# Four pairs of norm rows: 128-partition loads against one row, a product with ones and a ScalarE copy

## The chip, the cores and the metric

The kernel runs on one core of a Trainium2 chip, in float32 throughout. The metric is the device time of one execution in microseconds. Where several executions were timed, their median is given.

## The reference, cut to what matters

The model is a stack of two blocks on 256 tokens of width 1024. The first block (two hybrid layers) comes before the part in question. The second block has two layers, each an attention mixer and a mixture of 32 experts, of which every token takes two:

```python
for i in range(DEPTH):                       # DEPTH = 2
    mod = c_act @ ada_w[i] + ada_b[i]
    sh1, sc1, g1, sh2, sc2, g2 = jnp.split(mod[:, None, :], 6, axis=-1)
    h = x * (1 + sc1) + sh1
    y = mixer(h)                             # neighbourhood (i=0) or grouped-query (i=1)
    x = layer_norm(DEEPNORM_ALPHA * x + (1 + g1) * y, ln_g[i, 0], ln_b[i, 0])
    h = x * (1 + sc2) + sh2
    y = hierarchical_moe(h, ...)             # 32 experts, 1024 -> 512 -> 1024, gated by SiLU
    x = layer_norm(DEEPNORM_ALPHA * x + (1 + g2) * y, ln_g[i, 1], ln_b[i, 1])
```

`ln_g` and `ln_b` are rows of 1024 numbers, 4 KB each. A norm multiplies every token by the same row, and tokens lie on partitions, so the row is needed on all 128 partitions. There are four norms in the second block, so eight rows. Each expert has 6 MB of weights, 192 MB a layer, and all experts' weights are read.

## The kernel before, in words

One program is written out for each engine (TensorE, VectorE, ScalarE, GpSimd, SyncE); counting semaphores join them. Each engine works its own list strictly in order, so a wait holds up all that is behind it on that engine.

A layer of experts has this order. The mixer's output (`output(i)`) turns the tokens, computes the logits and normalizes. The `router(i)` picks the experts: on TensorE it makes the second gates (`second_gates`, a product of one row with ones, two halves in layer 0 and one in layer 1), then `busy`, a number of warming products whose results nobody reads (`busy(2 + i, 4)`; the profile shows two and three, as `busy` is called with i = 0 and 1), then, once VectorE has the choice (semaphore `asg`), the products that give each token its rank in an expert (`pos`) and the counts (`ct`). VectorE turns the ranks into a selection.

Then `experts(i)` goes over 8 quads of four experts (`q` from 0 to 7). A quad has a gather (tokens to expert slots, PSUM banks 0 and 1, taken out half by ScalarE and half by VectorE), the gate and up products (L910) of the four experts, turns of the hidden values (`hidden`), the gather of the next quad, two halves of down products (`down(0)`, `down(1)`, L946) and two of combining products (`combine`, L956). In the last quad the order is `down(0)`, `combine(0)`, `down(1)`, `combine(1)`.

The weights pass through nine slots of 2 MB: five of the tile `ring` and four in the arena `AR`. SyncE issues the loads in a fixed order and, for each, waits until the slot's former piece has been used. The plan `PARTS` lets the first three pieces of a layer free their slots in parts. The last quad's down weights are in pieces of 1 MB, by half.

The norm rows are loaded by GpSimd, whose queue has the function `small` for it (L2214). `norm_before(i)` loads the pair of the norm ahead of the experts (`LN_IN`: bias first, then scale), when the mixer's tokens are ready; `finish(i)` on GpSimd multiplies and adds them while the experts run, and signals `fin`. `norm_after(i)` loads the pair of the norm behind the experts (`LN_OUT`), scale when TensorE has filled the last gate products of quad 6, bias after those of quad 7; `last_norm(i)` on VectorE uses them. `LN_IN[1]`, `LN_OUT[0]` and `LN_OUT[1]` lie where gathered tokens lie at other times, `LN_IN[0]` where the scaled outputs lie. `begin` and `end` on TensorE reserve a PSUM bank and signal that it is filled; `free` signals that it is drained.

Of the kernel before, what the change touches and what calls it, by code (L numbers as in the profile page):

```python
# [10 lines left out]
ACT = mybir.ActivationFunctionType  # L11
AX = mybir.AxisListType.X

P = 128
NT = 2
D = 1024
# [114 lines left out]
def program(nc, A, out):  # L131
    with ExitStack() as ctx:
# [5 lines left out]
        def sem(name):  # L138
            if name not in sems:
                sems[name] = ctx.enter_context(nc.semaphore("s_" + name))  # L140
            return sems[name]
# [277 lines left out]
        def _(eng):  # L419
# [444 lines left out]
            def second_gates(i, j):  # L864
                pe.wait_ge(*drained("adaT", 12 * i + 10 + j))
                gate_rows("g2", i, 1, j, 1 if j and not i else 7)

            def router(i):
                for j in range(2 - i):
                    second_gates(i, j)  # L870
                busy(2 + i, 4)
                up = cst[:, K_UP:K_UP + 128]
                o = begin(4, "pos", i)
                pe.wait_ge(sem("asg"), i + 1)
                eng.matmul(o[:, 0:32], up, R_ASG[:, 0, :], start=True, stop=True)
                end(product(o[:, 32:64], [(up, R_ASG[:, 1, :]), (ones[:, :], R_ASG[:, 0, :])]), "pos", i)
                o = begin(7, "ct", i)
                end(product(o[:, 0:32], [(ones[:, :], R_ASG[:, 0, :]), (ones[:, :], R_ASG[:, 1, :])]), "ct", i)

            def experts(i):  # L880
# [9 lines left out]
                        end(ins, "xg", i, q, b)  # L890

                gather(0)
                for q in range(NQ):
                    u = q % 2

# [33 lines left out]
                    hidden(3)  # L929
                    if q + 1 < NQ:  # L930
                        gather(q + 1)

                    def down(n):
                        o = begin(5 + n, "dn", i, q, n)
# [24 lines left out]
                    down(0)  # L959
                    if q == NQ - 1:  # L960
                        combine(0)
                        down(1)
                    else:
                        down(1)
                        combine(0)
# [61 lines left out]
        def _(eng):  # L1027
# [794 lines left out]
            def last_norm(i):  # L1822
                for t in range(NT):
                    deviation(t)
                v.wait_ge(sem(f"row{2 * i + 1}"), 32)
                for t in range(NT):
                    v.step(stt(X[:, t, :], X[:, t, :], bn_a[:, t, 0:1], LN_OUT[0], ALU.subtract, ALU.mult))
                v.chain()
                for t in range(NT):
                    v.wait_ge(sem("lrs"), n_dev[0] - 1 + t)  # L1830
                    ins = stt(X[:, t, :], X[:, t, :], st2[:, t:t + 1], LN_OUT[1], ALU.mult, ALU.add)
                    if i + 1 < DEPTH:
                        v.tell(ins, sem("xn"), 3 + t)
                    else:
                        v.tell(ins, sem("xl"), t + 1)
# [12 lines left out]
        def _(eng):  # L1848
# [192 lines left out]
            def output(i):  # L2041
# [2 lines left out]
                raw_cols(i, 1)  # L2044
                normed(i, 1)

            def second_gates(i, j):
                s.wait_ge(*filled("g2", i, j))
                free(act(G2[j], bank("g2", i, j)[:, :], ACT.Copy), "g2", i, j)
# [82 lines left out]
            def router(i):  # L2132
                for j in range(2 - i):
                    second_gates(i, j)
                s.chain()
                eg, e2 = rt(104, NT, 4), rt(90, NT)
                s.wait_ge(sem("eg"), i + 1)
# [4 lines left out]
            def experts(i):  # L2142
# [12 lines left out]
                            s.step(ins)  # L2155

                gather(0)
                for q in range(NQ):
                    for j in range(4):
                        n = 32 * i + 4 * q + j  # L2160
# [7 lines left out]
                        second_gates(i, 1)  # L2168
                    if q + 1 < NQ:
                        gather(q + 1)  # L2170

            def overflow(i):
                o_pe, o_v, o_s = sem(f"o_pe{i}"), sem(f"o_v{i}"), sem(f"o_s{i}")
# [29 lines left out]
        def _(eng):  # L2203
# [20 lines left out]


            def norm_row(k, n, dst):
                small(dst, A[("ln_g", "ln_b")[n]][k // 2, k % 2:k % 2 + 1, :].to_broadcast([P, D]), f"row{k}")

            def norm_before(i):
                g.wait_ge(*drained("o", TAG[i], 7))  # L2230
# [16 lines left out]


            def finish(i):
                g.wait_ge(sem(f"row{2 * i}"), 32)  # L2250
                g.wait_ge(sem("sel"), 8 * i + 1)
                x = [X[:, t, :].rearrange("p (k c) -> p k c", c=NC) for t in range(NT)]
                for t in range(NT):
# [294 lines left out]
```

## Time and the profile before

| what | value |
|---|---|
| runs: median (lowest to highest of 3) | 1555.37 us (1554.26 to 1557.9) |
| profiled execution: span from first to last instruction | 1548.5 us |
| profiled execution: its own time | not listed in the views, which give its span alone |
| TensorE matmul, busy | 1384.9 us, 89% |
| VectorE busy | 563.6 us, 36% |
| ScalarE busy | 214.9 us, 14% |
| GpSimd busy | 88.4 us, 6% |
| DMA, hardware queue of SyncE | 519.40 MB, 83.2% of 16 engines |
| DMA, software queue of GpSimd | 11.95 MB, 2.2% of 16 engines |
| mean granted TensorE clock | 0.957 |

A product of float32 shows as two or more matmul instructions, and matmuls are pipelined, so TensorE's busy share says little by itself. A DMA share of one means that all 16 engines are working. PE is TensorE, PEld its weight loads, DVE VectorE, ACT ScalarE, POOL GpSimd, SPq SyncE's queue of instructions. A bracket after a row tells how long the engine idled before it and who ended that.

### The profile page before, as it was taken

Reading aid. Unit: us, or ns where it says so; the run is one execution under the profiler, and the core shown is the slowest. Engines: PE = TensorE matmul, PEld = TensorE weight load, DVE = VectorE, ACT = ScalarE, POOL = GpSimd, SP = SyncE. Lnnn points to the kernel's source line nnn. Section 1 sums busy time; section 2 is a strip of 40 time slices with the busy share of each in tenths; the row PEclk is TensorE's granted clock in tenths of the full one; section 3 lists DMA queues with packets and bytes.
Section 4 is the critical chain, followed back from the end, with each engine's and each line's share of the span. In section 5 each row is a group of like instructions: output and inputs, shape, how many; then the busy total and the mean of one; then the engine's idle time right before and its main releaser. Section 6 shows DMA issues by size and latency. Waiting matters only on the chain.

```text
span 1548.5 us, 28441 instructions
## 1 busy us (share of the span) xinstructions
PE 1384.9 (89%) x12810; PEld 880.9 (57%) x12810; DVE 563.6 (36%) x1254; ACT 214.9 (14%) x574; POOL 88.4 (6%) x95
## 2 busy tenths in 40 slices
PE   7999999999999999879879787879999798798795
PEld 4886478678886556435445343457765363454451
DVE  3696459656753321111111115794111111111113
ACT  2230123012332000000000002442100000000000
POOL 3100111000003000000000001100200000000000
PEclk9999999999999999989989899989999898899898
DMA  9656845767769999999999999357999999999995
GB/s 346 219 192 231 307 163 179 273 241 268 272 274 389 415 426 426 427 427 426 428 425 427 426 379 337 110 202 279 423 409 426 427 427 427 427 426 426 425 418 200
DMA packets 98296, 533.33 MB, mean 344 GB/s; under 512 B 5344, under 2 KB 7584, under 8 KB 74352
## 3 DMA queue, kind: packets, MB, share of 16 engines
q1 hardware_dynamic: 94432, 519.40, 83.2%
q0 software_dynamic: 3728, 11.95, 2.2%
q8 instruction: 105, 1.72, 0.4%
q14 instruction: 31, 0.25, 0.1%
HBM read 530.28 MB, written 1.05 MB: 343 GB/s over the span
## 4 chain that ended last, share of the span: by engine, by line
PE 66%; DMA 26%; DVE 4%; SPq 2%; issue 1%; ACT 1%; DVEq 0%; ACTq 0%
PE bk L438 28%; PE bk L910 17%; DMA ring<-in_moe_w_down 16%; DMA AR<-in_moe_w_down 9%; PE bk L946 8%; PE bk L619 4%; PE bk L956 4%; PE bk L434 2%; SPq L2356 2%; PE bk L648 1%; PE bk L663 1%; DVE AR L1031 1%; ACT AR L1852 1%; DMA ring<-in_w_in 1%; DVE AR L1039 1%
## 5 line engine op out<-in xcount | busy, mean ns | idle before, releaser
L910 PE MATMUL bk<-ring,AR 128*32 128x128 f32 x4480 | 267.7, 409 | 4.4 <-DMA ring<-in_moe_w_up 4.4
L1031 DVE TENSOR_TENSOR AR<-bk,AR 128x128 f32<-128x128 f32 (+2 forms) x106 | 41.3, 390 | 517.4 <-ACT AR L1852 451.5
L910 PEld LDWEIGHTS bk<-ring,AR 128*32 128x32 f32 x4480 | 178.8, 127 | 83.8 <-DMA ring<-in_moe_w_up 6.9
L910 PE MATMUL bk<-AR 128*32 128x128 f32 x3712 | 223.4, 409 | 3.5 <-DMA AR<-in_moe_w_up 2.8
L438 PE MATMUL bk<-ring,AR 128*128 128x256 f32 (+2 forms) x736 | 210.6, 444 | 6.5 <-ACT AR L1852 2.9
L946 PE MATMUL bk<-ring,AR 128*32 128x512 f32 x608 | 158.9, 696 | 51.4 <-DMA ring<-in_moe_w_down 50.6
L1852 ACT ACTIVATE AR<-bk 128x512 f32<-128x512 f32 (+4 forms) x178 | 72.0, 422 | 928.6 <-PE bk L910 757.5
L910 PEld LDWEIGHTS bk<-AR 128*32 128x32 f32 x3712 | 145.0, 127 | 74.1 <-DMA AR<-in_moe_w_up 5.9
L438 PEld LDWEIGHTS bk<-ring,AR 128*128 128x128 f32 x736 | 139.6, 192 | 71.4 <-issue 54.4
L946 PE MATMUL bk<-AR 128*32 128x512 f32 x416 | 149.6, 693 | 29.5 <-DMA AR<-in_moe_w_down 29.5
L438 PE MATMUL bk<-AR,ring 128*128 128x256 f32 (+1 forms) x832 | 170.5, 364 | 1.7 <-DVE AR L1036 1.4
L438 PEld LDWEIGHTS bk<-AR,ring 128*128 128x128 f32 x832 | 147.5, 190 | 21.6 <-issue 3.4
L946 PEld LDWEIGHTS bk<-ring,AR 128*32 128x32 f32 x608 | 35.0, 125 | 129.0 <-DMA ring<-in_moe_w_down 73.3
L1031 DVE TENSOR_TENSOR AR<-bk,mpart 128x512 f32<-128x512 f32 x32 | 22.1, 692 | 222.6 <-PE bk L946 222.6
L1039 DVE SCALAR_TENSOR_TENSOR mpart<-ring,ccol,mpart 128x512 f32<-128x512 f32 x126 | 98.7, 784 | 4.5
L434 PE MATMUL bk<-cst,AR 128*128 128x128 f32 (+1 forms) x356 | 63.9, 292 | 27.0 <-DVE AR L1699 11.8
L434 PEld LDWEIGHTS bk<-cst,AR 128*128 128x128 f32 (+1 forms) x356 | 41.3, 142 | 62.2 <-issue 26.2
L946 PEld LDWEIGHTS bk<-AR 128*32 128x32 f32 x416 | 31.8, 124 | 75.8 <-DMA AR<-in_moe_w_down 43.1
L438 PE MATMUL bk<-AR 128*128 128x128 f32 (+1 forms) x536 | 68.9, 286 | 1.0 <-DVE AR L1031 1.0
L438 PEld LDWEIGHTS bk<-AR 128*128 128x128 f32 x536 | 63.8, 193 | 5.2 <-issue 3.1
L956 PE MATMUL bk<-AR 128*128 128x512 f32 x128 | 59.7, 606 | 3.3 <-DVE AR L1031 3.3
L1031 DVE TENSOR_TENSOR X<-X,bk 128x512 f32<-128x512 f32 x64 | 44.0, 688 | 40.1 <-PE bk L619 23.9
(154 smaller groups left out, 947.9 us busy)
## 6 DMA issues: line engine op xcount, KB each, us to landing
ring<-in_moe_w_gate SPq DMA_DIRECT2D x36, 2048.0 KB, 28.8
ring<-in_moe_w_up SPq DMA_DIRECT2D x34, 2048.0 KB, 26.4
AR<-in_moe_w_up SPq DMA_DIRECT2D x30, 2048.0 KB, 29.7
AR<-in_moe_w_gate SPq DMA_DIRECT2D x28, 2048.0 KB, 26.8
ring<-in_moe_w_down SPq DMA_DIRECT2D x28, 2048.0 KB, 34.4
ring<-in_ada_w SPq DMA_DIRECT2D x24, 2048.0 KB, 10.8
AR<-in_moe_w_down SPq DMA_DIRECT2D x22, 2048.0 KB, 34.2
ring<-in_w_in SPq DMA_DIRECT2D x12, 2048.0 KB, 12.8
```

The costliest lines, as they stand in the source:

```text
L434: return eng.transpose(o, a, ident[0:k, 0:k])
L438: ins = eng.matmul(o, l, r, start=i == 0, stop=i == len(pairs) - 1)
L619: ins = eng.matmul(o[:, :], BIG[:, x, OUTS[m] + 128 * t:OUTS[m] + 128 * t + 128], w[:, 2 * m + x, :], start=k + x == 0, stop=k + x == 4)
L648: ins = eng.matmul(o[b][:, a * nk:(a + 1) * nk], g["q"][h][:, t * 128:(t + 1) * 128], g["k"][h][:, 0:nk], start=True, stop=True)
L663: ins = eng.matmul(o[64 * b:64 * b + 64, 128 * x:128 * x + 128], g["v"][2 * x + b][kt], ET[j % 2][:, (2 * b + x) * nkt + kt, :], start=kt ...
L910: ins = eng.matmul(o[32 * f:32 * f + 32, 128 * m:128 * m + 128], XG[u][:, c, 32 * j:32 * j + 32], w[:, c, f::4], start=c == 0, stop=c == N ...
L946: ins = eng.matmul(o[32 * j:32 * j + 32, :], AT[u][:, j, 32 * f:32 * f + 32], w, start=f == 0, stop=f == 3)
L956: end(eng.matmul(o[:, :], GST[u][:, 128 * t:128 * t + 128], YS[:, 512 * n:512 * n + 512], start=True, stop=True), "cb", i, q, n, t)
L1031: return eng.tensor_tensor(o, a, b, op)
L1039: return eng.scalar_tensor_tensor(out=o, in0=a, scalar=s, in1=b, op0=op0, op1=op1)
L1852: return eng.activation(o, a, f, **kw)
L2356: eng.dma_start(dst, src).then_inc(sem(f"slot{s}"), 16)
```

## The change

The eight rows are no longer loaded to 128 partitions, 512 KB each. GpSimd loads each to partition 0 alone, 4 KB, at the same places of its list. TensorE multiplies a column of ones with the row, in two halves of 512 columns, which puts the row on all partitions of a PSUM bank, and ScalarE copies each half to the place where the 512 KB load put it. The users (`finish`, `last_norm`) wait for these copies. On TensorE the pairs of products stand: LN_IN[1] in the router behind the second gates, with one warming product fewer; LN_IN[0] behind the first gather; LN_OUT[0] behind the last quad's hidden values, ahead of `down(0)`; LN_OUT[1] between `combine(0)` and `down(1)` of the last quad.

```diff
--- before.py
+++ after.py
@@ -865,10 +865,18 @@
                 pe.wait_ge(*drained("adaT", 12 * i + 10 + j))
                 gate_rows("g2", i, 1, j, 1 if j and not i else 7)
 
+            def norm_row(k, w, dst, banks_):
+                for h in range(2):
+                    o = begin(banks_[h], "row", k, w, h)
+                    pe.wait_ge(sem("ones"), 1)
+                    pe.wait_ge(sem(f"row{k}{w}"), 16)
+                    end(eng.matmul(o[:, :], ones[0:1, :], dst[0:1, 512 * h:512 * h + 512], start=True, stop=True), "row", k, w, h)
+
             def router(i):
                 for j in range(2 - i):
                     second_gates(i, j)
-                busy(2 + i, 4)
+                norm_row(2 * i, 1, LN_IN[1], (0, 1))
+                busy(1 + i, 4)
                 up = cst[:, K_UP:K_UP + 128]
                 o = begin(4, "pos", i)
                 pe.wait_ge(sem("asg"), i + 1)
@@ -890,6 +898,7 @@
                         end(ins, "xg", i, q, b)
 
                 gather(0)
+                norm_row(2 * i, 0, LN_IN[0], (2, 3))
                 for q in range(NQ):
                     u = q % 2
 
@@ -929,6 +938,8 @@
                     hidden(3)
                     if q + 1 < NQ:
                         gather(q + 1)
+                    else:
+                        norm_row(2 * i + 1, 0, LN_OUT[0], (0, 1))
 
                     def down(n):
                         o = begin(5 + n, "dn", i, q, n)
@@ -959,6 +970,7 @@
                     down(0)
                     if q == NQ - 1:
                         combine(0)
+                        norm_row(2 * i + 1, 1, LN_OUT[1], (0, 1))
                         down(1)
                     else:
                         down(1)
@@ -1822,7 +1834,9 @@
             def last_norm(i):
                 for t in range(NT):
                     deviation(t)
-                v.wait_ge(sem(f"row{2 * i + 1}"), 32)
+                for n in range(2):
+                    for h in range(2):
+                        v.wait_ge(*drained("row", 2 * i + 1, n, h))
                 for t in range(NT):
                     v.step(stt(X[:, t, :], X[:, t, :], bn_a[:, t, 0:1], LN_OUT[0], ALU.subtract, ALU.mult))
                 v.chain()
@@ -2044,6 +2058,12 @@
                 raw_cols(i, 1)
                 normed(i, 1)
 
+            def norm_row(k, w, dst):
+                for h in range(2):
+                    s.wait_ge(*filled("row", k, w, h))
+                    ins = act(dst[:, 512 * h:512 * h + 512], bank("row", k, w, h)[:, :], ACT.Copy)
+                    free(ins, "row", k, w, h)
+
             def second_gates(i, j):
                 s.wait_ge(*filled("g2", i, j))
                 free(act(G2[j], bank("g2", i, j)[:, :], ACT.Copy), "g2", i, j)
@@ -2132,6 +2152,8 @@
             def router(i):
                 for j in range(2 - i):
                     second_gates(i, j)
+                s.wait_ge(*filled("row", 2 * i, 1, 0))
+                norm_row(2 * i, 1, LN_IN[1])
                 s.chain()
                 eg, e2 = rt(104, NT, 4), rt(90, NT)
                 s.wait_ge(sem("eg"), i + 1)
@@ -2155,6 +2177,7 @@
                             s.step(ins)
 
                 gather(0)
+                norm_row(2 * i, 0, LN_IN[0])
                 for q in range(NQ):
                     for j in range(4):
                         n = 32 * i + 4 * q + j
@@ -2168,6 +2191,8 @@
                         second_gates(i, 1)
                     if q + 1 < NQ:
                         gather(q + 1)
+                norm_row(2 * i + 1, 0, LN_OUT[0])
+                norm_row(2 * i + 1, 1, LN_OUT[1])
 
             def overflow(i):
                 o_pe, o_v, o_s = sem(f"o_pe{i}"), sem(f"o_v{i}"), sem(f"o_s{i}")
@@ -2224,7 +2249,7 @@
 
 
             def norm_row(k, n, dst):
-                small(dst, A[("ln_g", "ln_b")[n]][k // 2, k % 2:k % 2 + 1, :].to_broadcast([P, D]), f"row{k}")
+                small(dst[0:1, :], A[("ln_g", "ln_b")[n]][k // 2, k % 2:k % 2 + 1, :], f"row{k}{n}")
 
             def norm_before(i):
                 g.wait_ge(*drained("o", TAG[i], 7))
@@ -2247,7 +2272,9 @@
 
 
             def finish(i):
-                g.wait_ge(sem(f"row{2 * i}"), 32)
+                for n in range(2):
+                    for h in range(2):
+                        g.wait_ge(*drained("row", 2 * i, n, h))
                 g.wait_ge(sem("sel"), 8 * i + 1)
                 x = [X[:, t, :].rearrange("p (k c) -> p k c", c=NC) for t in range(NT)]
                 for t in range(NT):
```

## Rows read from the trace of the kernel before

**Rows 1.** The page: mean busy share of the DMA engines in 40 equal slices
```profile
DMA  9656845767769999999999999357999999999995
```

**Rows 2.** The chain that ended last, in layer 0 (start us, us, what)
```profile
483.34 3.81 PE bk L438 x32
...
487.15 14.91 PE bk L910 x235
...
523.47 7.00 PE bk L946 x64
...
592.22 36.43 DMA AR<-in_moe_w_down
```

**Rows 3.** Windows: length, busy us (x count) by engine, then granted clock, DMA share, GB/s
```profile
525.00:530.00 5.00, 5.00 (x52) 1.43 (x44) 0.69 (x1) 0.00 (x0) 0.00 (x0) 1.00 1.01 426
...
530.00:535.00 5.00, 5.00 (x36) 2.11 (x32) 3.44 (x5) 0.00 (x0) 0.00 (x0) 1.00 0.88 328
...
1130.00:1135.00 5.00, 5.00 (x32) 2.04 (x28) 3.45 (x5) 0.00 (x0) 0.00 (x0) 1.00 0.80 285
...
1525.00:1530.00 5.00, 3.98 (x10) 0.96 (x10) 2.68 (x5) 0.00 (x0) 0.00 (x0) 1.00 0.54 201
```

**Rows 4.** SyncE's issues in time, layer 0 (start us, us, engine, line, operation)
```profile
488.24 10.49 SPq L2352 DMA_DIRECT2D ring<-in_moe_w_down  x8
...
517.68 0.33 SPq L2356 DMA_DIRECT2D AR<-in_moe_w_gate  x1
...
530.53 0.33 SPq L2356 DMA_DIRECT2D AR<-in_moe_w_up  x1
```

**Rows 5.** GpSimd's issues of the rows, in time
```profile
474.34 0.57 POOL L2214 DMA_DIRECT2D AR<-in_ln_b  x1
...
851.31 0.59 POOL L2214 DMA_DIRECT2D AR<-in_ln_g  x1 [348.20 <-PE bk L910]
...
912.53 0.53 POOL L2214 DMA_DIRECT2D AR<-in_ln_b  x1 [60.62 <-PE bk L910]
...
1074.06 0.59 POOL L2214 DMA_DIRECT2D AR<-in_ln_b  x1
```

**Rows 6.** DMA: GpSimd's queue in 1440 to 1549; loads with landing; ada_b_g's rows' landing
```profile
q0 software_dynamic: 288, 1.05, 2.4%
...
AR<-in_ln_b POOLq DMA_DIRECT2D x4, 512.0 KB, 9.4
...
cst<-in_ln_g POOLq DMA_DIRECT2D x1, 16.0 KB, 2.3
...
DMA to landing us min/median/max: 6.4/6.8/7.1
```

**Rows 7.** TensorE in time, router of layer 0
```profile
477.49 1.98 PE L672 MATMUL bk<-grow,ones 1*128 1x512 f32 x4
...
479.39 1.98 PE L862 MATMUL bk<-cst 128*128 128x512 f32 x4
...
481.55 0.41 PE L875 MATMUL bk<-AR,cst 128*128 128x32 f32 x2 [0.17 <-DVE AR L1031]
```

**Rows 8.** TensorE in time, router of layer 1
```profile
1077.33 2.84 PE L862 MATMUL bk<-cst 128*128 128x512 f32 x6
...
1081.28 0.41 PE L875 MATMUL bk<-AR,cst 128*128 128x32 f32 x2 [1.11 <-DVE AR L1031]
```

**Rows 9.** ScalarE in time: a gate half's copy out of PSUM
```profile
478.64 0.60 ACT L1852 ACTIVATE mpart<-bk 128x512 f32<-128x512 f32 x1 [1.78 <-PE bk L672]
```

**Rows 10.** TensorE in time, end of quad 7 of layer 0
```profile
914.14 0.33 PE L434 MATMUL bk<-cst,AR 128*128 128x128 f32 x1 [0.52 <-DVE AR L1731]
...
920.39 0.62 PE L946 MATMUL bk<-ring,AR 128*32 128x512 f32 x2 [2.07 <-DMA ring<-in_moe_w_down]
...
928.47 0.62 PE L946 MATMUL bk<-ring,AR 128*32 128x512 f32 x1
...
930.95 0.62 PE L946 MATMUL bk<-ring,AR 128*32 128x512 f32 x2 [1.42 <-DMA ring<-in_moe_w_down]
```

## The prediction

> **What bounds the kernel now.** I read the DMA line of the page first [rows 1]. Its two long runs of nines belong to the experts, where the weights come in. The reader's first idea is then: bytes taken away there are time taken away. The chain of waits [rows 2] corrects this for the beginning of each expert stage. From 483 us to 592 us the chain of layer 0 holds only TensorE pieces; the first long DMA piece is the one at 592.22, the down weights of quad 2. So quads 0 and 1 are paced by TensorE, the quads from 2 on by DMA.
>
> The windows [rows 3] show where one hands over to the other. DMA runs at 426 GB/s up to 530, falls to 328 GB/s in 530 to 535 (layer 1: 285 GB/s in 1130 to 1135), and is full afterwards. The missing part is (426-328)/426 x 5 = 1.15 us in layer 0 and (426-285)/426 x 5 = 1.65 us in layer 1: DMA has run dry there. SyncE's issues say why [rows 4]: no issue between 517.68 and 530.53, the time at which TensorE ends the down products of quad 0 (523.47 + 7.00 = 530.47 [rows 2]) and frees slots. The stage thus has two parts. Up to about 530.5 its clock is TensorE's way from the router to the end of quad 0. What is issued from 530.53 on is a fixed number of bytes, moved at full rate up to the end. The layer's end is the first time plus those bytes, and a load that ends before 530.5 is not among them.
>
> **The change part by part.**
>
> *Scale and bias before the experts (LN_IN).* Two loads of 512 KB, the first issued at 474.34 (layer 1: 1074.06) [rows 5], become two of 4 KB. One load costs this much of the DMA engines: in the window that holds the two late loads, their queue took 2.4% of 109 us, so 2.6 us for two, 1.3 us each [rows 6] (by bytes at 426 GB/s: 1.23 us). Taking 2.6 us from 474 to 490 is worth nothing here: DMA reaches the refills that TensorE releases (first at 488.24 [rows 4]) earlier and waits longer, or runs dry earlier than 530. I take 0; the other bound is -2.6 us a layer, if DMA and not TensorE set quad 0.
>
> In its place TensorE gets four products of one row with 512 columns, two per row of parameters. The kernel has the same product already: two gate halves at 477.49, four instructions, next work at 479.39, so 0.95 us each [rows 7]. One pair is 1.9 us. A warming product costs the same 0.95 us (479.39 to 481.3 for two), and one of them is dropped.
>
> The first pair (LN_IN[1]) stands in the router ahead of the products of the ranks, on TensorE's way. It must first wait until its row has landed. Behind it in TensorE's order are the warming products, the ranks, the first gather, and all of quad 0. Ranks start now at 481.55 after 0.17 us of waiting (layer 1: 1081.28, after 1.11 us) [rows 7, 8]. When does a 4 KB row land? No such load runs at this point, so I bound it: 2.3 us from issue (the 16 KB load of ln_g, early in the kernel) and 9.4 us (median of the four 512 KB loads of ln_b). Nearest are the four 4 KB rows of ada_b_g, the same queue under full DMA load: 6.4 to 7.1 us, median 6.8 [rows 6]. Those stood behind other loads of their queue, and this one is the first of its queue, so I take their lowest, 6.4.
>
> - Layer 0: landed at 474.34 + 6.4 = 480.74; the gates end at 479.4, so TensorE stands 1.3 us. Then 1.9 + one warming product 0.95 gives 483.6 against 481.55: late by 2.0 us.
> - Layer 1: landed at 1074.06 + 6.4 = 1080.46; the gate ends at 1077.3 [rows 8]. Then 1.9 + two warming products 1.9 gives 1084.3 against 1081.28: late by 3.0 us.
> - With 2.3 us the row is there first: 479.4 + 2.85 = 482.25, late by 0.7; layer 1 1077.33 + 3.8 = 1081.1, late by 0. With 7.1 us: 2.7 and 3.7. With 9.4 us: 5.0 and 6.0.
>
> The row shows 6.4 us and more under load. The Trainium skill (DMA: Bandwidth & Descriptors, section "Anatomy of one DMA — SWDGE (gpsimd) path") gives a fit of 2.0 us plus bytes over 436 GB/s for a load from this queue, so 2.0 us for 4 KB; by it the router would be late by 0.7 and 0 us as with the 2.3 us load, and my total below 4.3 us lower. The profile's loaded rows decide for me.
>
> The second pair (LN_IN[0]) stands between the first gather and the gate products of quad 0. The gather ran from 483.34 for 3.81 us and the gate products begin where it ends, at 487.15 [rows 2], so the full 1.9 us is added, in each layer. Its row was issued right after the other and has landed by then. Together TensorE ends quad 0 later by 2.0 + 1.9 = 3.9 us (layer 0) and 3.0 + 1.9 = 4.9 us (layer 1): 8.8 us.
>
> ScalarE's copies cost 0.60 us for 128 x 512 [rows 9]: 1.2 us a pair. In the router they come before its two exponentials, which VectorE wants only after its own first selection, which is itself later by the same delay; after the gather they come before the first SiLU, which needs a whole expert's gate products. If ScalarE had no such room it would be 1.2 us a layer. GpSimd's finish waits for the second copy instead of the 512 KB load; its end is wanted by the second gather, which comes after all gate products of quad 0: 0.
>
> *Scale and bias after the experts (LN_OUT).* Two more 512 KB loads a layer vanish; one was issued when TensorE ended the gate products of quad 6 (851.31), the other after quad 7 (912.53), before the last weights landed (930.95 [rows 10]). Both lie in the stretch that DMA paces, so both are gained in full: 2.6 us a layer, 5.2 us (by bytes 4.9; lower bound 0, if something else sets the end).
>
> TensorE's two pairs here lie beside DMA waits. The first, ahead of down(0), starts at 914.5 and takes 1.9 us, or 3.8 at half the clock. Down(0) waited until 920.39 for its last piece, 2.07 us of idling inside its first round: hidden. The second pair stands between combine(0) and down(1), which begins at 928.47 and idles 1.42 us for the last piece at 930.95 [rows 10]. 1.9 us is more than 1.42, but the products ahead of this wait run beside those of the last piece when all has landed: a half of down takes 3.5 us (7.00 for both [rows 2]), so 928.47 + 1.9 + 3.5 = 933.9, still before 930.95 + 3.5 = 934.45, where it ends now; the landings of both halves' last pieces move together. I take 0, bound +0.5 us a layer. The last row is issued at 912.5 and wanted at 928.5. The copies come beside down(1) and its combining, ahead of the last norm.
>
> **Sum.** +8.8 (TensorE up to the end of quad 0) - 5.2 (bytes after it) = +3.6 us on a span of 1548.5, 1552.1. The views give no time of the profiled execution but its span; the median of the runs, 1555.37, lies 6.9 us above it, and I keep that: 1559.0 us. From no change a measurement can tell about 0.2%, 3.1 us; 3.6 is only just beyond.
>
> **The rivals.**
> - *The rows land early* (2.3 us). Then 0.7 + 0 + 3.8 - 5.2 = -0.7 us, 1554.7, no difference. For it: a 4 KB row puts little on each engine. Against it: the four 4 KB rows under load.
> - *DMA sets the stage all along*, the side opposite to mine. All eight loads count, 8 x 1.3 = 10.5 us, and TensorE's products vanish in waits: 1544.9. It decides if DMA doesn't run dry at the end of quad 0. Against it: the two dips [rows 3], the 13 us without an issue [rows 4], and a chain without DMA before 592.
> - *Late rows.* At 7.1 us and with 0.5 a layer at the end: 2.7 + 3.7 + 3.8 + 1.0 - 5.2 = +6.0 us, 1561.4. At 9.4 us it would be 5.0 + 6.0 + 3.8 - 5.2 = +9.6.
> - *The end doesn't follow the bytes*: the last landing is that of one late engine and doesn't move. Then the 5.2 us stay: +8.8, 1564.2. For it: in 1525 to 1530 DMA is half empty [rows 3] though the last piece has still to land. Against it: this load's packets lie on every engine, also on the late one.
>
> **Chances and range.** Forecast 0.58, its own range 1556.5 to 1560.5; about 0.35 of it lies above 3.1 us and 0.23 below. Rows early 0.13 (same). DMA all along 0.07 (faster). Late rows 0.14 (slower). End not following 0.08 (slower). So faster 0.07, same 0.36, slower 0.57. The range 1554.3 to 1562.0 leaves out the second and the last rival, 0.15, and takes in the bounds of landing from 2.3 to a little over 7.1 us.
>
> **What would show it.** In the profile after: GpSimd's queue moves about 4 MB less; the ranks' products start 2 to 3 us later counted from the issue of the row, with a wait of TensorE for the ln_b row just before; the first gate product 3.9 and 4.9 us later; the dip in DMA at the end of quad 0 unchanged in size, with a new one around 488 to 494, before the first refill; from there to the end of the layer 2.6 us less. I am wrong if the row lands in under 4 us, if there is no new dip and the old one vanishes, or if the stretch from quad 0's end to the last landing keeps its length.

## The result, and the profile after

The kernel after the change took 1566.37 us (median; 1563.1 to 1569.13 in 8 runs), the kernel before 1556.52 us beside it (1550.07 to 1560.02). The ratio is 1.0072 with an interval of 1.0053 to 1.0091, so the change costs 11.2 us (8.2 to 14.2). I had forecast +3.6 us, range 1554.3 to 1562.0. The sign is right; the size is three times too small.

From the page of the kernel after: the span, TensorE's busy time, the DMA share in 40 slices, and GpSimd's queue (packets, MB, share of 16 engines).

```profile
span 1564.9 us, 28526 instructions
...
PE 1408.3 (90%) x12838; PEld 890.6 (57%) x12838; DVE 563.3 (36%) x1254; ACT 224.4 (14%) x590; POOL 88.1 (6%) x95
...
DMA  9556845768766999999999999257799999999995
...
q0 software_dynamic: 2832, 7.79, 1.5%
```

GpSimd's queue moves 4.2 MB less (7.79 against 11.95), as the change intends, and TensorE is busy 23 us longer, though eight pairs less two warming products make only 13.3 us (8 x 1.9 - 2 x 0.95). The missing 10 us are the first sign of what I had left out: the same instructions last longer.

I count each layer from the issue of its ln_b row ahead of the experts. GpSimd's issues in time, kernel after, layers 0 and 1:

```profile
475.68 0.54 POOL L2239 DMA_DIRECT2D AR<-in_ln_b  x1
```
```profile
1084.52 0.56 POOL L2239 DMA_DIRECT2D AR<-in_ln_b  x1
```

TensorE in time, kernel after, router of layer 0 up to the first gate products (answers to [rows 2, 7]):

```profile
478.83 1.98 PE L672 MATMUL bk<-grow,ones 1*128 1x512 f32 x4
481.99 3.18 PE L873 MATMUL bk<-AR,ones 1*128 1x512 f32 x4 [1.17 <-DMA AR<-in_ln_b]
485.10 2.08 PE L862 MATMUL bk<-cst 128*128 128x512 f32 x2
486.96 0.47 PE L883 MATMUL bk<-AR,cst 128*128 128x32 f32 x2
...
489.23 5.54 PE L438 MATMUL bk<-AR 128*128 128x128 f32 x32
494.70 1.98 PE L873 MATMUL bk<-AR,ones 1*128 1x512 f32 x4
496.61 11.21 PE L919 MATMUL bk<-ring,AR 128*32 128x128 f32 x192
```

The same for layer 1 (answers to [rows 8]):

```profile
1089.99 3.60 PE L873 MATMUL bk<-AR,ones 1*128 1x512 f32 x4 [2.12 <-DMA AR<-in_ln_b]
1093.52 3.71 PE L862 MATMUL bk<-cst 128*128 128x512 f32 x4
1097.07 0.30 PE L883 MATMUL bk<-AR,cst 128*128 128x32 f32 x2
...
1098.75 3.81 PE L438 MATMUL bk<-AR 128*128 128x128 f32 x32 [0.49 <-DVE AR L1043]
1102.49 1.98 PE L873 MATMUL bk<-AR,ones 1*128 1x512 f32 x4
```

The reader is to see two things. TensorE does wait for the row (1.17 and 2.12 us), as forecast. And the four instructions of a pair take 3.18 and 3.60 us here, against 1.98 us for the same pair behind the gather and for the gates before it; the two warming instructions 2.08 us instead of 1.0; the gather of layer 0 5.54 us instead of 3.81. The windows say why (length, busy us and count of PE, PEld, DVE, ACT, POOL, then granted clock, DMA share, GB/s; kernel after, answers to [rows 3]):

```profile
480.00:485.00 5.00, 3.83 (x6) 0.85 (x4) 2.63 (x16) 1.78 (x3) 0.00 (x0) 0.76 1.00 424
485.00:490.00 5.00, 4.92 (x17) 3.68 (x16) 1.50 (x10) 0.90 (x3) 0.00 (x0) 0.50 0.90 383
490.00:495.00 5.00, 5.00 (x31) 4.87 (x31) 0.23 (x2) 1.50 (x4) 0.00 (x0) 0.71 0.01 3
...
540.00:545.00 5.00, 5.00 (x40) 2.26 (x42) 3.26 (x5) 0.00 (x0) 0.00 (x0) 1.00 0.92 324
...
1090.00:1095.00 5.00, 5.00 (x6) 1.81 (x7) 1.68 (x10) 1.50 (x4) 0.00 (x0) 0.52 1.00 429
```

The granted clock is 0.50 in 485 to 490, the lower of TensorE's two levels (1.2 GHz against 2.4), and was 1.00 in all windows of the kernel before from 480 to 500. Counted from record to record, the lower level holds for 10.2 us in layer 0 and 6.8 us in layer 1; in the profile of before it does not occur in a router. DMA stands empty at 490 to 495, where it had 390 GB/s before: the new dip. The dip at the end of quad 0 is still there, 324 GB/s against 328.

The layer's end in the kernel after, in the chain of waits (answers to [rows 10]):

```profile
928.58 5.91 PE bk L957 x26
935.34 1.96 PE bk L967 x4
937.30 1.91 PE bk L873 x4
939.21 3.62 PE bk L957 x32
```

`down(1)` starts at 939.21 straight behind the pair and waits for no weights; before, it idled 1.42 us for the last piece. But by the trace that piece landed at 939.05, only 0.1 us before the products that need it: weights and TensorE arrive together here. The last combining product starts 5.84 us behind the last landing in both layers before, and 5.94 and 5.84 us behind it after.

| us after the issue of ln_b | before, layer 0 / 1 | after, layer 0 / 1 | later by |
|---|---|---|---|
| ranks start | 7.21 / 7.22 | 11.28 / 12.55 | 4.07 / 5.33 |
| gather starts | 9.00 / 9.02 | 13.55 / 14.23 | 4.55 / 5.21 |
| first gate product | 12.74 / 12.76 | 20.93 / 19.88 | 8.19 / 7.12 |
| from it to the last combining | 448.27 / 448.85 | 446.98 / 447.55 | -1.29 / -1.30 |

The traces differ by 8.19 + 7.12 - 2.6 = 12.7 us in the stretches that the change touches, which fits the 11.2 of the timed runs. The spans differ by 16.4 us; of the other 3.7, 1.3 lie ahead of the first issue (475.68 - 474.34) and nearly all the rest between the end of layer 0 and the next issue, outside the experts. The profiled execution of before was a quick one: with the 1.7 to 1.9 us by which every timed run on record exceeds its span, it took 1550.2 to 1550.4 us, near the lowest of its runs.

### The profile page after: what moved, and what is told of

It reads as the page before. It is cut to its first block, busy times and chain, and to the rows that moved or that the text cites. A ratio compares the mean times of both kernels' runs of the same rounds, so it can differ in the third digit from the quotient of the medians.

```text
span 1564.9 us, 28526 instructions
## 1 busy us (share of the span) xinstructions
PE 1408.3 (90%) x12838; PEld 890.6 (57%) x12838; DVE 563.3 (36%) x1254; ACT 224.4 (14%) x590; POOL 88.1 (6%) x95
## 3 DMA queue, kind: packets, MB, share of 16 engines
q0 software_dynamic: 2832, 7.79, 1.5%
## 4 chain that ended last, share of the span: by engine, by line
PE 67%; DMA 26%; DVE 3%; SPq 1%; ACT 1%; issue 1%; DVEq 0%; POOL 0%; ACTq 0%
PE bk L438 27%; PE bk L919 17%; DMA ring<-in_moe_w_down 16%; DMA AR<-in_moe_w_down 9%; PE bk L957 9%; PE bk L967 4%; PE bk L619 4%; PE bk L434 2%; PE bk L648 1%; PE bk L663 1%; SPq L2383 1%; ACT AR L1866 1%; PE bk L873 1%; DVE AR L1043 1%; DMA AR<-in_ln_b 1%
## 5 line engine op out<-in xcount | busy, mean ns | idle before, releaser
L1866 ACT ACTIVATE AR<-bk 128x512 f32<-128x512 f32 (+3 forms) x194 | 81.7, 436 | 950.1 <-PE bk L919 755.0
L438 PE MATMUL bk<-AR 128*128 128x128 f32 (+1 forms) x536 | 72.2, 295 | 0.6 <-DVE AR L1043 0.5
L438 PEld LDWEIGHTS bk<-AR 128*128 128x128 f32 x536 | 67.1, 202 | 4.8 <-issue 2.7
```

Source lines behind the costliest of these rows:

```text
L438: ins = eng.matmul(o, l, r, start=i == 0, stop=i == len(pairs) - 1)
L1866: return eng.activation(o, a, f, **kw)
```

## The experiments

All ratios are against the kernel before, run on the same chip; us are the ratio's excess times that median. "Stretch" is the table's last line, "router" its third. Three suspects for the lower clock are told apart: the wait for the row, the one-row products, and the mere length of the chain of small work. Beside it stands the question what the bytes bring.

**in_only: the LN_IN half alone.** LN_OUT's rows are loaded as before.

```diff
-                norm_row(2 * i + 1, ...)                 # TensorE and ScalarE, both
+                v.wait_ge(sem(f"row{2 * i + 1}"), 32)    # rows to 128 partitions again
```


> Only the four rows ahead of the experts are changed; the rows behind them are loaded as before. Clock theory: between the issue of the bias row and the first gate product lie 12.7 us before and 20.9 and 19.9 us after the whole change, of which 3.5 us more than forecast come from products at half clock; the same should show here, a granted clock of 0.5 for 7 to 10 us in both routers and +7 to +8 us a layer, +13 to +16 us in all, since the bytes saved ahead of the end of quad 0 bring nothing. Rival (the harm lies at the end of the stage, where a pair stands on the chain of waits): here only +4 to +9 us.

Measured: 1571.64 us, ratio 1.0116 (1.0097 to 1.0135), +18.0 us. Router 21.70 and 22.99 us, so 9.0 and 10.2 later than before; lower clock for 13.7 us in both layers, gathers 5.52 and 5.61 us. In layer 0 the clock fell at 477.2, among the gates and ahead of the wait for the row. All of the loss lies in this half.

**out_only: the LN_OUT half alone.** The router is that of before.

```diff
-                norm_row(2 * i, 1, LN_IN[1], (0, 1))
-                busy(1 + i, 4)
+                busy(2 + i, 4)
...
-                norm_row(2 * i, 0, LN_IN[0], (2, 3))
```


> Only the four rows behind the experts are changed. From the traces of before and after, the stretch from the first gate product to the last combining is 1.3 us shorter in each layer, so -2.6 us, between -1 and -4. Rival (the end of the stage is where the harm lies): slower than before, by 1 to 6 us. Rival (all bytes gained, products hidden): -5.2 us.

Measured: 1550.31 us, ratio 0.9981 (0.9963 to 0.9999), -3.0 us. Stretches 445.68 and 446.21, so 2.6 less in each layer, the forecast size. TensorE in time, and a window at the last quad of layer 0:

```profile
916.28 1.07 PE L955 MATMUL bk<-ring,AR 128*32 128x512 f32 x2 [0.75 <-DMA ring<-in_moe_w_down]
```
```profile
915.00:920.00 5.00, 4.25 (x23) 0.99 (x24) 0.00 (x0) 0.00 (x0) 0.00 (x0) 0.50 1.05 381
```

Here too `down(0)` runs at the lower clock, behind a pair and a wait for weights, and the 2.6 us come all the same.

**bytes_in, bytes_out: the row alone, no pairs.** Each takes the kernel before and loads two of the four rows of a layer to partition 0 only, with no product that spreads them.

```diff
-                small(dst, src.to_broadcast([P, D]), f"row{k}")
+                small(dst[0:1, :], src, f"row{k}")       # k even (in) or odd (out)
```


> The kernel before, in which the two loads ahead of the experts bring one row to one partition and nothing spreads it: the first norm's scale and bias are wrong on 127 partitions, everything else is computed. Theory (TensorE paces the stage up to the end of quad 0): 0 us, within 1, and the dry place of DMA at the end of quad 0 grows from 1.2 and 1.7 us by some 2.5 us a layer, or one opens ahead of the first refill. Rival (bytes count everywhere): -5.2 us.

> The kernel before, in which the two loads behind the experts bring one row to one partition and nothing spreads it: the second norm's scale and bias are wrong on 127 partitions. Theory (both loads lie in the stretch that DMA paces): -2.6 us a layer, -5.2 us in all (4.9 by bytes). Rival (the last landing is that of one late engine and does not move, or TensorE paces the end): 0 to -2.6 us.

Measured: 1712.63 and 1703.78 us. The other partitions held old numbers, the tokens went to other experts, and a branch for overflowing experts ran that the kernel otherwise skips (each trace has three more loads of experts' weights, at the end). Nothing about bytes follows from these totals. The next two replace the rows' use by constants.

**bytes_in2, bytes_out2: the same, norm with 1 and 0.**

```diff
+        unit = sb("unit", [P, 1, 1]); nought = sb("nought", [P, 1])
-                ... LN_IN[0] ... ALU.mult      /  ... LN_IN[1], ALU.add
+                ... unit ...     ALU.mult      /  ... nought,   ALU.add
```


> The kernel before, in which the two loads ahead of the experts bring 4 KB to one partition, nothing spreads it, and the norm is computed with scale 1 and bias 0 from constant tiles (so that the experts' loads stay nearly the same; the output is not the reference's). Theory (TensorE paces the stage up to the end of quad 0): 0 us, within 1.5, and DMA runs dry some 2.5 us longer a layer, ahead of the first refill or at the end of quad 0. Rival (bytes count everywhere): -5.2 us.

> The kernel before, in which the two loads behind the experts bring 4 KB to one partition, nothing spreads it, and the norm is computed with scale 1 and bias 0 from constant tiles (the output is not the reference's). Theory (both loads lie in the stretch that DMA paces): -2.6 us a layer, -5.2 us in all (4.9 by bytes). Rival (TensorE or one late engine paces the end): 0 to -2.6 us.

Measured, bytes_out2: 1550.2 us, ratio 0.9970 (0.9955 to 0.9984), -4.7 us (-7.0 to -2.5). The 5.2 us of the forecast for the bytes by themselves lie inside the interval, and the rival's 0 to -2.6 almost wholly outside it. By the traces the stretches are 2.4 and 0.8 us shorter. Its router is that of before, and yet fell to the lower clock for 10.2 us in layer 0 in the profiled execution (more below).

Measured, bytes_in2: 1556.09 us, ratio 1.0009 (0.9994 to 1.0025), +1.4 us, though it only takes work away. All engines in time:

```profile
481.61 4.91 POOL L2209 TENSOR_TENSOR X<-AR,unit 128x1024 f32<-128x1024 f32 x2 [7.97 <-issue]
...
481.65 2.43 DVE L1033 TENSOR_TENSOR AR<-AR 128x2 f32<-128x2 f32 x1
...
484.19 4.36 DVE L1033 TENSOR_TENSOR AR<-AR 128x16 f32<-128x16 f32 x3
...
490.01 9.41 PE L912 MATMUL bk<-ring,AR 128*32 128x128 f32 x160 [2.64 <-DVE AR L1038]
```

GpSimd's `finish` no longer waits for a late load, so it starts at 481.61, beside VectorE's last small operations for the router. A product of two columns takes VectorE 2.43 us (0.16 in the kernel before), the time of one of GpSimd's two instructions (4.91 for both), and three more take 4.36 (0.57 before). VectorE then comes late to take the gathered tokens out of PSUM. The router is as long as before, but TensorE idles 2.64 us for these tokens among its first gate products. The Trainium skill (SBUF — State Buffer, section "SBUF: two separate sides") says that a GpSimd operation and a VectorE operation with two SBUF inputs lock a shared pair of ports, whole instruction by whole instruction; the trace agrees, with 2.43 us for two columns. So this kernel measured a new collision, not the bytes; its stretches are 3.5 and 2.9 us longer than before.

**bytes_in3: bytes_in2 with `finish` held back** to the first gate products.

```diff
                 g.wait_ge(sem("sel"), 8 * i + 1)
+                g.wait_ge(*filled("gu", i, 0, 0))
```


> As the kernel with 4 KB loads ahead of the experts, scale 1 and bias 0, but GpSimd's finish waits for the first expert's gate and up products, so that it starts at about its old time (5 us behind the first gate product) and not 4 us ahead of it, where it held VectorE's copies up for 2.6 us. Theory (TensorE paces the stage up to the end of quad 0): first gate product to first combining product 43.3 and 43.7 us as before, to last combining product 448 us, 0 us in all within 1.5. Rival (bytes count everywhere): 2.6 us less a layer.

Measured: 1553.03 us, ratio 0.9998 (0.9983 to 1.0013), -0.3 us (-2.6 to +2.0). Router 12.74 and 12.75, stretches 448.52 and 449.00, as before. Windows of bytes_in3:

```profile
485.00:490.00 5.00, 5.00 (x63) 4.35 (x65) 1.90 (x9) 2.79 (x5) 0.00 (x0) 1.00 0.86 365
490.00:495.00 5.00, 5.00 (x92) 3.25 (x88) 0.66 (x5) 0.00 (x0) 0.00 (x0) 1.00 0.76 228
...
530.00:535.00 5.00, 5.00 (x24) 1.70 (x16) 2.57 (x4) 0.00 (x0) 0.00 (x0) 1.00 0.89 344
```

The bytes spared ahead of quad 0 come back as DMA standing idle at 485 to 495 (365 and 228 GB/s, where the kernel before has 442 and 390). They are worth nothing, as forecast.

**early_row: is it the wait?** The ln_b row's load moves ahead of a piece of the norm's work, so that TensorE need not wait for it.

```diff
             deviation(0)
+            g.wait_ge(*drained("o", TAG[0], 7))
+            norm_row(0, 1, LN_IN[1])
             deviation(1)
```


> The whole change, with one move: the bias row ahead of the experts is issued some 18 us earlier (ahead of the second rsqrt of the mixer's norm), so that TensorE finds it landed in the router. The products of one row stay where they are. Theory W (it is the wait for the row that lets TensorE's clock fall): no row of granted clock 0.5 in the routers, first gate product 0.7+1.9 and 0+1.9 us later than before, in all +4.5 - 2.6 = about +2 us on the kernel before. Theory K (products of one row do not keep the clock up, waited for or not): the clock still falls to 0.5, the pairs take more than 3 us, and the total stays at +8 to +11.

Measured: 1561.13 us, ratio 1.0031 (1.0013 to 1.0048), +4.8 us. Times from here on for the early kernels are counted from the ln_g row. Router 20.78 and 17.91. TensorE in time, layer 0, and windows, layers 0 and 1:

```profile
475.95 0.69 PE L672 MATMUL bk<-grow,ones 1*128 1x512 f32 x1
475.96 0.69 PE L873 MATMUL bk<-AR,ones 1*128 1x512 f32 x1
...
476.91 1.80 PE L672 MATMUL bk<-grow,ones 1*128 1x512 f32 x2
479.40 2.07 PE L873 MATMUL bk<-AR,ones 1*128 1x512 f32 x2 [0.69 <-ACT mpart L1866]
481.40 2.07 PE L862 MATMUL bk<-cst 128*128 128x512 f32 x2
...
485.53 6.25 PE L438 MATMUL bk<-AR 128*128 128x128 f32 x32
```
```profile
477.00:478.00 1.00, 1.00 (x4) 0.14 (x1) 0.86 (x5) 0.60 (x1) 0.00 (x0) 0.50 1.03 428
...
1082.00:1084.00 2.00, 2.00 (x7) 0.75 (x7) 1.72 (x9) 1.16 (x4) 0.00 (x0) 1.00 0.97 411
1084.00:1086.00 2.00, 2.00 (x4) 0.55 (x3) 1.66 (x11) 0.55 (x2) 0.00 (x0) 0.64 1.00 427
```

No wait for the row is left, and the lower level holds for 13.7 and 10.2 us all the same. The wait alone is not the cause. With the row there early, the first half of the pair runs beside a gate half, 0.01 us behind it (475.95 and 475.96; in layer 1 1081.82 and 1081.83): both are products of one row, of rows on different partitions. In layer 0 it even runs ahead of the second gate half, which stands before it in TensorE's list; so for products on different rows the list is not worked strictly in order. In layer 1 TensorE works without a gap through gate and pair, and the clock falls just behind them, at 1084.6. In layer 0 it falls at 477.0, at the end of these two; the second half of the pair then waits 0.69 us for ScalarE's copy of the last gate half, whose bank it uses.

**dense: the router's pair with all 128 rows.** Its contraction runs over 128 partitions instead of one; the other pairs stay as they are. What it adds up is no longer the row, so the tokens go to other experts and the branch for overflow runs; only the router of its trace is of use.

```diff
+                    r = P if k % 2 == 0 and w else 1
-                    ... ones[0:1, :], dst[0:1, ...]
+                    ... ones[0:r, :], dst[0:r, ...]
```


> The whole change with its wait for the row, but the pair in the router multiplies all 128 rows of its tile with 128 x 128 ones instead of one row with one column (the bias of the norm ahead of the experts is then a sum over partitions and wrong; all else is computed, though the choice of the second layer's experts may shift). Theory W: as the whole change, clock 0.5 for 7 to 10 us in both routers, +11. Theory K: the clock stays at 1.0 or falls for less than 4 us; the rest, late row and added products, is 8.8 - 2.6 = +6.

Measured: ratio 1.139 (1.1366 to 1.1415), not usable. Lower clock for 6.8 and 3.4 us against 10.2 and 6.8 in the kernel after; both gathers 3.81 us; router 19.01 and 18.24. Less of it, not none.

**warm_first: warming ahead of the pair.**

```diff
-                norm_row(2 * i, 1, LN_IN[1], (0, 1))
-                busy(1 + i, 4)
+                busy(2 + i, 4)
+                norm_row(2 * i, 1, LN_IN[1], (0, 1))
```


> The whole change with the warming products ahead of the router's pair instead of behind it, and none dropped (two and three): the wait for the row is filled with them. Theory W: TensorE idles no more than 0.3 us ahead of the pair, the clock stays up, and the first gate product comes 0.9+1.9 and 1.2+1.9 us later than before: in all +6 - 2.6 = +3 us. Theory K: the clock falls during or behind the pair, 3 to 8 us at 0.5 in each router, +6 to +11.

Measured: 1559.51 us, ratio 1.0022 (1.0005 to 1.0040), +3.4 us. Router 20.87 and 18.31, gathers 6.71 and 6.72 us. It fills the wait, so ranks come 10.54 and 7.95 us after the issue, and both pairs run at the full clock (1.98 us). But in layer 0 the clock is low for 3.4 us among gates and warming, ahead of the pair, and in both layers for 6.8 us behind it, and both gathers pay.

**out_best: out_only with its pairs moved** out of the two places at the layer's end.

```diff
+                        if q + 2 == NQ:                          # behind the last gather
+                            norm_row(2 * i + 1, 0, LN_OUT[0], (2, 3))
...
                     combine(1)
+                norm_row(2 * i + 1, 1, LN_OUT[1], (0, 1))
```


> Only the rows behind the experts are changed, and their pairs stand elsewhere: the scale's behind the gather of the last quad, in quad 6, where TensorE waits 8 us and more for down weights, and the bias's behind the last combining product; the last norm waits for each just before it uses it. All bytes gained and no product on the chain of waits: first gate product to last combining 2.6 us shorter in each layer, -5.2 us (by bytes 4.9). Rival (the pair at the end costs even here, through the norm that waits for its copies): -5.2 + 2 x 1 = -3 us, no better than the kernel that changed only these rows.

Measured: 1553.46 us, ratio 0.9986 (0.9972 to 1.0), -2.2 us. Not told apart from out_only.

**early_sel, wait_sel: is it the one row?** `first` is a tile whose row 0 is one and all else zero. A product over 128 rows with it gives the same row on all partitions, whatever the other rows hold. wait_sel is the kernel after with this; early_sel is early_row with this.

```diff
-                    end(eng.matmul(o[:, :], ones[0:1, :], dst[0:1, 512 * h:512 * h + 512], ...
+                    end(eng.matmul(o[:, :], first[:, :], dst[:, 512 * h:512 * h + 512], ...
```


> The whole change with the early bias row, and every pair multiplies all 128 rows of its tile with a 128 x 128 matrix whose first row is ones and the rest zeros: the same result and the same columns, with all rows of the array at work. Theory L (one-row products and waits both leave the array idle, and a stretch of either or both lets the clock fall): no 0.5 in the routers now, first gate product +15.3 and +14.7 us after the bias row's old place of issue (before: 12.74 and 12.76), the sum +4.5 less 2.6 to 5.2 for the bytes behind: -0.7 to +1.9 us on the kernel before. Theory K2 (what lets the clock fall is the length of the router's small work, whatever the pair is): the clock falls in or behind it, +3 to +7.

> The whole change with its wait for the row in the router, and the 128-row products of the kernel beside it. Theory L: gates and wait together let the clock fall once ahead of the pair, but the products that follow bring it back by the gather (3.8 us for 32 instructions); first gate product +18.5 and +17.8 us as with the sum over partitions (19.0 and 18.2), +11.3 less 2.6 to 5.2: +6 to +9 us. Rival (the wait costs only its own length): +4 us.

Measured, early_sel: 1550.85 us, ratio 0.9976 (0.9960 to 0.9992), -3.7 us (-6.2 to -1.2). TensorE in time and windows, layer 0:

```profile
478.12 1.98 PE L874 MATMUL bk<-AR,first 128*128 128x512 f32 x4
479.94 1.02 PE L863 MATMUL bk<-cst 128*128 128x512 f32 x2
...
482.48 3.81 PE L439 MATMUL bk<-AR 128*128 128x128 f32 x32 [0.49 <-DVE AR L1044]
```
```profile
475.00:480.00 5.00, 5.00 (x15) 2.03 (x15) 3.90 (x22) 2.39 (x4) 0.00 (x0) 1.00 1.02 430
480.00:485.00 5.00, 4.51 (x35) 3.95 (x34) 2.07 (x13) 1.35 (x5) 0.00 (x0) 1.00 1.00 429
```

A pair takes 1.98 us, no more than with one row at full clock, and the clock does not fall in either layer. Router 14.85 and 14.42 us against 20.78 and 17.91 in early_row: 9.4 us in two layers by the traces, 8.5 us by the ratios, 12 runs each. The programs differ in the number of rows alone. The chain of small work is no shorter, so its length is not the cause: a product with 128 rows does not run beside the gate, and the pair begins where the gates end. The clock was recorded in every timed run, not only in the profiled one: its mean over a run lies between 0.946 and 0.955 in the twelve of early_row and between 0.958 and 0.964 in the twelve of early_sel.

Measured, wait_sel: 1557.97 us, ratio 1.0028 (1.0011 to 1.0046), +4.4 us (1.7 to 7.2). TensorE in time and windows, layer 0:

```profile
480.98 3.78 PE L874 MATMUL bk<-AR,first 128*128 128x512 f32 x4 [0.70 <-DMA AR<-in_ln_b]
...
488.02 3.81 PE L439 MATMUL bk<-AR 128*128 128x128 f32 x32 [0.49 <-DVE AR L1044]
```
```profile
480.00:485.00 5.00, 4.30 (x6) 1.85 (x6) 1.96 (x12) 1.39 (x3) 0.00 (x0) 0.50 1.01 430
485.00:490.00 5.00, 4.51 (x30) 3.50 (x29) 1.61 (x10) 0.70 (x3) 0.00 (x0) 0.86 0.71 305
```

With the wait back, the clock falls again, for 6.8 and 3.4 us (in layer 0 at 479.6, among the one-row gates; in layer 1 in the wait), but has come back by the gather. So both the wait and the one-row products count: rows alone bring 11.2 down to 4.4, rows and early load to -3.7.

**out_warm: out_only with a warming product behind each gate.**

```diff
                 for j in range(2 - i):
                     second_gates(i, j)
-                busy(2 + i, 4)
+                    busy(4 if i else 1, 4)
```


> Only the rows behind the experts are changed, as in the kernel that changed them alone, and the warming products of the router stand between the gate halves in layer 0 (gate, warm, gate, warm) and number four instead of three in layer 1, where 1.1 us are free. Profiles of kernels with an unchanged router show the clock fall in one router of the two now and then (gather 5.1 to 5.3 us instead of 3.8). If that is the difference between runs, this kernel has no such fall and its runs lie closer together, at the fast end: -5.2 - 1 = -6 us. Rival (no such link): as the kernel without it, -3 us.

Measured: 1550.1 us, ratio 0.9971 (0.9955 to 0.9986), -4.5 us (-7.0 to -2.2). Its profiled router of layer 0 had the lower clock for 13.7 us, so it does not do what it was built for; the total is not told apart from out_only's.

**out_sel: out_only with 128-row products.**

> Only the rows behind the experts are changed, as in the kernel that changed them alone, and their pairs use all 128 rows of the array (first row ones, the rest zeros). The first pair lies where the clock falls at the end of a layer (0.5 to 0.7 for 3 to 7 us). Theory L: with full rows the clock stays up there in more layers, first gate product to last combining product 445.5 to 446.5 us in both, the total -5 to -6 us on the kernel before. Rival (the end is paced by the last landing alone): no different from the one-row form, 445.7 and 446.2 us, -3 us.

Measured: 1552.13 us, ratio 0.9983 (0.9963 to 1.0002), -2.6 us (-5.7 to +0.3). The clock stays at 1.00 through the last quad's down products in both layers, where out_only had 6.8 and 3.5 us at the lower level. In the time this does not show: not told apart from out_only either, since the end there follows the last landing (5.84 us behind it in both layers).

## Why the prediction was wrong

**Where the forecast held.** The quads up to 0 are TensorE's and the later ones DMA's: bytes ahead of quad 0 brought -0.3 us and bytes behind it -4.7 us when taken away by themselves (bytes_in3, bytes_out2). The rival in which DMA sets the stage all along is out. The row under load: the pair began 6.31 and 5.47 us after the issue, against 6.4 taken from [rows 6]. The fit of the Trainium skill (DMA: Bandwidth & Descriptors, section "Anatomy of one DMA — SWDGE (gpsimd) path"), 2.0 us for 4 KB, is not borne out here; the medians of the eight rows are 5.4 and 6.4 us. TensorE stood 1.17 us for it in layer 0 and 2.12 in layer 1 (forecast 1.3 and 3.1). The second pair cost 1.91 us in each layer. The new dip of DMA is where I put it. The rival that came nearest, "the end doesn't follow the bytes" (+8.8 us), would have been near by luck: the bytes behind were gained (bytes_out2), and the last combining products start 5.8 to 5.9 us behind the last landing before and after.

**The step that failed.** It is "Then 1.9 + one warming product 0.95 gives 483.6" and its twin for layer 1. I took the time of one product, 0.95 us, from [rows 7], where the clock is full, and used it behind a wait and behind one-row products. The runs show in its place:

| term | forecast, layer 0 / 1 | measured |
|---|---|---|
| wait, beyond the gates' end | 1.3 / 3.1 | 1.3 / 2.2 |
| first pair | 1.9 / 1.9 | 3.1 / 3.5 |
| warming left, less warming before | -0.95 / -0.95 | -0.1 / 0.7 |
| wait ahead of the ranks, gone | -0.2 / -1.1 | -0.2 / -1.1 |
| ranks to gather | 0 / 0 | 0.5 / -0.1 |
| gather | 0 / 0 | 1.7 / 0 |
| second pair | 1.9 / 1.9 | 1.9 / 1.9 |

Up to the first gate product that makes 15.3 us instead of 8.8, an excess of 6.5. I priced the lower clock at the layer's end ("or 3.8 at half the clock"), where it was hidden, and not in the router, where it is not.

**What keeps the clock low.** Shown by the timed runs: with the load early and no wait for it, one-row products cost 8.5 us more than products over 128 rows of the same duration. With 128-row products the wait costs 8.1 us (+4.4 against -3.7), of which some 2.2 are the wait itself (1.3 - 0.2 and 2.2 - 1.1 in the table). With both it is +11.2, so the two don't add up; together they hold the lower level longest (10.2 and 6.8 us in the kernel after, 6.8 and 3.4 in wait_sel, where it is over by the gather). What starts a fall is not shown: in layer 0 of in_only, warm_first, wait_sel, dense and bytes_out2 it began among the gates, which every kernel has, ahead of pair and wait.

One profile of a kernel says less here than it seems. Routers that are the same as before had it in some profiled executions: none in before and bytes_in3, 3.4 us in one layer each of out_only, out_best, out_sel and bytes_in2, 10.2 us in one of bytes_out2: 24 us in 14 layers, 1.7 us a layer. With one-row pairs in the router (after, in_only, early_row, warm_first) it was 85 us in 8 layers, 10.7 a layer. The change makes a thing long and regular that was short and came now and then. That it also makes up the spread of the kernel before (1548 to 1561 us) fits its recorded clocks, whose mean is 0.958 in the 14 runs below 1551 us and 0.951 in the 34 above 1557; no run here was made for it.

**The smaller error.** Behind the first gate product I forecast -2.6 us a layer, and the kernel after has -1.3. Over the ten kernels whose LN_OUT rows are short (dense left out) this stretch was 0.75 to 2.95 us shorter than before, mean 1.9; in in_only and bytes_in3, with LN_OUT as before, it was 0.2 to 1.4 us longer. So 1.3 is inside the scatter. The missing part lies ahead of the pairs: the last weights landed only 1.4 and 1.3 us earlier behind the first gate product, and from there to the last combining products nothing changed by more than 0.1 us. In out_only the pairs stood beside the same lower clock and 2.6 came in full. So the pairs at the end are not the cause; why the weights came 1.3 us later than forecast stays open.

**Around the span.** I added 6.9 us, the median less the span. In all timed runs on record the time lies 1.7 to 1.9 us above the span; the rest of the 6.9 is that the profiled execution of before was a quick one. As the forecast was a difference on the median, this did no harm.

## What to carry to other kernels

A duration read at full clock holds for an instruction that is moved only if what stands ahead of it still keeps the clock up: when an edit puts a wait or products with few rows into a chain of small work, price all of it up to the next long products at both levels. A row can be spread over partitions by a product with a 128-row selector at the same 1.98 us as with one row of ones; with the load issued early enough, this turned +11.2 us into -3.7. Take bytes away where DMA sets the pace and nowhere else: here the 2 MB behind gave 4.7 us and the 2 MB ahead none.

## What the runs showed of the hardware

- Four matmul instructions with a contraction of one row and 512 columns last 1.98 us, as with 128 rows, but keep up the granted clock less well (mean over a run 0.946 to 0.955 in early_row, 0.958 to 0.964 in early_sel). In early_row it fell at 1084.6, after TensorE had been busy 2.00 of 2.00 us in each window from 1080. The Trainium skill (TensorE: Matmul & The Clock Gate, section "Part 1: The HAM clock gate") ties the clock to how busy TensorE has been. By the profile's busy share this trace does not agree.
- Two one-row products whose rows lie on different partitions (the gate's on 32 or 96, the pair's on 0) ran at the same time in early_row: the pair's two instructions began 0.01 us behind the gate's and lasted as long, 0.69 and 0.59 us. In layer 0 they began ahead of the second gate half (476.91), which comes before them in the program.
- The eight 4 KB loads from GpSimd's queue in the kernel after were there after 5.2 to 6.9 us, those in the routers beside full weight traffic. The 512 KB loads of ln_b took 11.6 and 12.3 us in the routers of before and 7.2 and 6.9 at the layers' ends; the 9.4 of [rows 6] is the median of these four.
- A GpSimd product over 128x1024 beside VectorE's small ones cost TensorE 2.64 us among the first gate products (bytes_in2). Where `finish` waited for slow loads, that wait had kept the two apart.
